# Two further matmuls behind each group of one-column modulation sums, in a one-core transformer kernel

## The chip, the cores and the metric

The kernel runs on one NeuronCore of a Trainium2 chip. The metric is device time in microseconds (us) of one execution, median of several. TensorE (PE) multiplies, VectorE (DVE) and ScalarE (ACT) prepare its operands and take its results out of PSUM, SyncE (SP) issues nearly all transfers from HBM.

## The reference, cut to what matters

Two transformer blocks run one after the other on 256 tokens of width 2048, batch 1, float32. The first block is a hybrid mixer (gated delta rule and convolution), cross attention to a memory of 256 tokens and a squared-ReLU MLP of width 8192. The second is a block whose norms and residuals are modulated by vectors that come from conditioning inputs:

```python
mod_in = jax.nn.silu(c)
modc_in = jax.nn.silu(c_ctx)
sh1, sc1, gt1, sh2, sc2, gt2 = jnp.split((mod_in @ w_mod[l] + b_mod[l])[:, None, :], 6, axis=-1)
csh1, csc1, cgt1, csh2, csc2, cgt2 = jnp.split(modc_in @ w_mod[l] + b_mod[l], 6, axis=-1)
h = rmsnorm(x, g_attn[l]) * (1 + sc1) + sh1
```

The matrix `w_mod` is 2048 x 12288 and multiplies single vectors, while every other matrix multiplies 256 tokens.

## The kernel before, in words

All dense layers are one stream. The weights of every layer lie in HBM as 906 slots of 128 x 1024 float32. SP loads a slot into one of 8 raw buffers. ACT rounds it to `whi` (float32r), DVE subtracts to get the remainder `wlo` (L1218), each with 4 buffers, and PE uses the slot in 24 matmuls of 256 columns: for each 128 x 128 block of weights the three products whi x act[0], whi x act[1] and wlo x act[0], where `act[0]` and `act[1]` are the rounded activations and their remainder. All of them are recorded at line L448. In nearly all phases the weights are the stationary operand and `act` (or `hid`, for the second matrix of an MLP) is the moving one. In phases marked `flip` (memv, nav_c, nav_x, v_c, v_x) they change places: `act` is stationary and `whi` or `wlo` is moving.

The phases follow each other in the order of `phases()`: glu, qkv, z, then the delta rule, wout, memk, memv, wq, cross attention, wo, then w1 and w2 four times, then the second block. PE waits at the start of a slot for `split_done` (the slot is rounded and subtracted) and at the start of a block of outputs for `block_free` (its PSUM bank, 0 or 1, was read).

The product with `w_mod` is done by DVE beside the phases memk to w2_3. These have two loop bodies each, of 16 slots or 384 matmuls, 24 bodies in all. In a body DVE accumulates 512 modulation columns into `modacc` (L1202, L1204), for both vectors in the first 8 bodies (`mod=2`) and for one in the other 16 (`mod=1`). What is left is a sum over the 128 partitions. PE does it in `mod_matmuls`, after slot 12 of the next body: 8 or 4 matmuls whose stationary operand is 128 columns of `modacc` and whose moving operand is one column of ones, into bank 2. They are plain float32, and each has two records in the trace. Behind them the last 3 slots (72 matmuls) of the body follow, then the next phase or body. Bank 7 isn't used in the phases of these bodies but for the attention behind wq, which overwrites what it reads.

`act_skew` (448 bytes) and `h_skew` (64 bytes) are unused columns of SBUF that shift `act` and what lies behind it against the weights' buffers.

Of the kernel before, what the change touches and what calls it, by code (L numbers as in the profile page):

```python
# [14 lines left out]
P = 128  # L15
D = 2048
T = 256
# [110 lines left out]
def build(nc, x_t, mem_t, ctx_t, stream, mods, pvec, eye, cmix, catt, na_bias, na_mask, out_t):  # L128
    es = ExitStack()
    with es:  # L130
        def sb(name, shape, dt=F32, stack=None):
            return (stack or es).enter_context(nc.sbuf_tensor(name, shape, dt))
# [9 lines left out]
        act = sb("act", [P, 2, DC, T], F32R)  # L142
# [14 lines left out]
        with ExitStack() as first:  # L157
# [9 lines left out]
            with ExitStack() as mlp:  # L167
                hid = sb("hid", [P, 2, DC, T], F32R, stack=mlp)
# [32 lines left out]
        bank = [es.enter_context(nc.psum_tensor(f"bank{i}", [P, 512], F32)) for i in range(8)]  # L201
# [217 lines left out]
        def _(pe):  # L419
            c = Counts(pe)  # L420

            def phase(ph, src, c0=0, after=None):
# [3 lines left out]
                def body(i):  # L426
                    for k in range(ph.K):
                        b = bank[(ph.block0 + k) % 2]

                        pe.wait_ge(block_free, i * ph.K + (ph.block0 + k + 1))  # L430
                        for sl in range(ph.slots_per_block):
                            j = k * ph.slots_per_block + sl

                            pe.wait_ge(split_done, i * ph.S + (ph.slot0 + j + 1 + RAW_N))
                            if after and k == 0:
                                c.at(after[0], after[1] + (sl + 1) * after[2])
                            buf = (ph.slot0 + j) % SPL_N
                            for ci in range(ph.per_slot):
                                kc = sl * ph.per_slot + ci
                                for hf in range(ph.ncol // P if not ph.flip else TT):  # L440
                                    for n, (wx, ax) in enumerate(((whi, 0), (whi, 1), (wlo, 0))):
                                        if ph.flip:
                                            lhs = src[:, ax, c0 + kc, hf * P:(hf + 1) * P]
                                            rhs = wx[:, buf, ci * NCOL:(ci + 1) * NCOL]
                                        else:
                                            lhs = wx[:, buf, ci * ph.ncol + hf * P:ci * ph.ncol + (hf + 1) * P]
                                            rhs = src[:, ax, c0 + kc, :]
                                        mm = pe.matmul(b[:, hf * T:(hf + 1) * T], lhs, rhs,  # L448
                                                       start=(kc == 0 and hf == 0 and n == 0),
                                                       stop=(kc == ph.chunks - 1 and n == 2), skip_group_check=True)  # L450
                            mm.then_inc(slot_used, 1)
                            if ph.mod and j == MOD_OUT_AT:
                                mod_matmuls(ph, i)
# [3 lines left out]
            def mod_matmuls(ph, i):  # L457

                mb = i + ph.mod0
                pe.wait_ge(mod_used, mb * 8 + (8 + MOD_N))  # L460
                for w in range(ph.mod):
                    for n in range(MOD_COL // P):
                        mm = pe.matmul(bank[2][:, 4 * w + n:4 * w + n + 1], modacc[:, w, n * P:(n + 1) * P],  # L463
                                       ones[:, 0:1], start=True, stop=True, skip_group_check=True)
                mm.then_inc(mod_out, 1)

            def row_sums(out, src, tok, start, stop):

                return pe.matmul(out, src[:, tok], ones[:, 0:1], start=start, stop=stop, skip_group_check=True)  # L469
# [55 lines left out]
            for q in range(DC // 4):  # L525
                c.at(normed, q + 1)
                for k in range(4 * q, 4 * q + 4):
                    for mt in range(TT):
                        mm = pe.matmul(bank[4][:, 16 * mt:16 * mt + 16], tmp[:, k, mt * P:(mt + 1) * P],
                                       cc(CM, "w_ba")[:, 16 * k:16 * k + 16], start=(k == 0 and mt == 0), stop=(k == DC - 1),  # L530
                                       skip_group_check=True)
# [258 lines left out]
            for n in range(1 + MLA_H // 2):  # L790
                src = kr[:, 0, :] if n == 0 else qR[:, n - 1, :]
# [1079 lines left out]
```

## Time and profile before

| | |
|---|---|
| median of 3 runs | 3073.99 us (3073.78, 3073.99, 3084.93) |
| the profiled execution, its own time | 3077.71 us |
| its span, first to last instruction | 3075.9 us |
| mean granted TensorE clock | 0.970 of 2.4 GHz |
| busy: PE, weight loads, DVE, ACT | 94%, 92%, 68%, 43% |
| HBM traffic | 588 MB, 192 GB/s over the span |

All durations below come from the one profiled execution, which lies 3.7 us above the median. A matmul's record is longer than its share of the stream, since consecutive ones overlap: the distance between starts is the pace, and the length of a record is more than twice as long.

### The profile page before, as it was taken

The numbers are of one execution on the slowest core, as the hardware profiler recorded it, in microseconds if no ns is written. First come the engines' busy times: TensorE is split into PE (matmuls) and PEld (weight loads), VectorE is DVE, ScalarE is ACT, GpSimd is POOL, SyncE is SP. The second block draws the span as 40 slices with busy tenths as digits, with TensorE's granted clock in tenths as the row PEclk, the third lists the DMA queues.
The fourth block names the chain that finished last, engine by engine and source line by source line (L and its number), as shares of the span: only waits on it lengthen the run. The fifth ranks groups of instructions, "written<-read, shape, count | busy, mean of one in ns | idle before, by whom it ended". The sixth has DMA issues, their size and how long they took to land.

```text
span 3075.9 us, 55206 instructions
## 1 busy us (share of the span) xinstructions
PE 2901.8 (94%) x23858; PEld 2838.5 (92%) x23858; DVE 2096.0 (68%) x2934; ACT 1331.7 (43%) x1646; POOL 5.1 (0%) x13
## 2 busy tenths in 40 slices
PE   7998888999999899999999989988998999999998
PEld 7998787999998899999999979967598999999998
DVE  6988654698977877676766775454457665665665
ACT  4445323443433453444435444434345543554453
POOL 0000000000000000000000000000000000000000
PEclk9999898999999999999999989998999999999999
DMA  5554102577664677777777745522144565555553
GB/s 203 188 169 165 55 1 80 204 254 260 245 227 168 240 289 275 280 274 268 287 268 267 282 140 178 190 98 96 55 156 153 195 199 196 191 195 196 192 195 117
DMA packets 160451, 591.58 MB, mean 192 GB/s; under 512 B 17840, under 2 KB 17840, under 8 KB 159696
## 3 DMA queue, kind: packets, MB, share of 16 engines
q1 hardware_dynamic: 159264, 579.93, 53.4%
q0 software_dynamic: 944, 8.12, 0.7%
q8 instruction: 188, 3.08, 0.4%
q14 instruction: 55, 0.45, 0.1%
HBM read 585.88 MB, written 2.10 MB: 191 GB/s over the span
## 4 chain that ended last, share of the span: by engine, by line
PE 86%; DVE 10%; ACT 2%; issue 1%; DMA 1%; SPq 0%; DVEq 0%; ACTq 0%
PE bank L448 76%; DVE wlo L1218 2%; PE bank L712 1%; DVE ev L1237 1%; DVE modacc L1423 1%; PE bank L469 1%; PE bank L463 1%; PE bank L616 1%; PE bank L473 1%; DVE tmp L1373 1%; PE bank L614 1%; PE bank L608 1%; DVE ev L1340 1%; PE bank L687 1%; ACT whi L823 1%
## 5 line engine op out<-in xcount | busy, mean ns | idle before, releaser
L448 PE MATMUL bank<-act,whi 128*128 128x256 f32 x10144 | 1784.4, 281 | 59.7 <-DVE wlo L1218 20.2
L448 PEld LDWEIGHTS bank<-act,whi 128*128 128x128 f32 x10144 | 1560.0, 191 | 65.4 <-issue 34.1
L1218 DVE TENSOR_TENSOR wlo<-raw,whi 128x1024 fp32r<-128x1024 f32 x906 | 1098.1, 1223 | 530.2 <-ACT whi L823 528.4
L448 PE MATMUL bank<-act,wlo 128*128 128x256 f32 x5072 | 1421.7, 280 | 0.0
L823 ACT ACTIVATE whi<-raw 128x1024 fp32r<-128x1024 f32 x906 | 948.2, 1057 | 898.0 <-PE bank L448 897.4
L448 PEld LDWEIGHTS bank<-act,wlo 128*128 128x128 f32 x5072 | 969.4, 191 | 0.0
L448 PE MATMUL bank<-hid,whi 128*128 128x256 f32 x3456 | 602.5, 279 | 0.0
L448 PEld LDWEIGHTS bank<-hid,whi 128*128 128x128 f32 x3456 | 524.5, 188 | 0.0
L448 PE MATMUL bank<-hid,wlo 128*128 128x256 f32 x1728 | 482.1, 279 | 0.0
L1204 DVE SCALAR_TENSOR_TENSOR modacc<-modraw,small,modacc 128x512 f32<-128x512 f32 x480 | 348.6, 747 | 11.0 <-DMA modraw<-mods 5.6
L448 PEld LDWEIGHTS bank<-hid,wlo 128*128 128x128 f32 x1728 | 328.8, 190 | 0.0
L448 PE MATMUL bank<-whi,act 128*128 128x256 f32 x896 | 158.1, 279 | 0.0
L448 PEld LDWEIGHTS bank<-whi,act 128*128 128x128 f32 x896 | 136.5, 188 | 0.0
L448 PE MATMUL bank<-wlo,act 128*128 128x256 f32 x448 | 125.0, 279 | 0.0
L1293 DVE SCALAR_TENSOR_TENSOR ev<-bank,pv,ev 128x255 f32<-128x255 f32 x176 | 76.9, 478 | 62.8 <-ACT ev L888 61.3
L1423 DVE SCALAR_TENSOR_TENSOR modacc<-modraw,modacc 128x256 f32<-128x256 f32 x232 | 98.6, 481 | 0.1
L448 PEld LDWEIGHTS bank<-wlo,act 128*128 128x128 f32 x448 | 84.1, 188 | 0.0
L888 ACT ACTIVATE ev<-bank,pv 128x256 f32<-128x256 f32 x88 | 45.0, 561 | 70.4 <-PE bank L448 70.4
L901 ACT ACTIVATE ev<-h 128x512 f32<-128x512 f32 x40 | 25.3, 632 | 113.6 <-DVE h L1268 68.0
L1282 DVE TENSOR_TENSOR hid<-ev,hid 128x512 fp32r<-128x512 f32 x32 | 22.2, 693 | 72.8 <-ACT hid L877 72.8
L893 ACT ACTIVATE ev<-ev 128x256 f32<-128x256 f32 x44 | 18.4, 419 | 80.1 <-DVE ev L1293 80.1
L1014 ACT ACTIVATE tmp<-bank 128x512 f32<-128x512 f32 x28 | 16.7, 597 | 73.6 <-PE bank L608 73.6
(269 smaller groups left out, 1545.3 us busy)
## 6 DMA issues: line engine op xcount, KB each, us to landing
raw<-stream SPq DMA_DIRECT2D x906, 512.0 KB, 4.4
modraw<-mods SPq DMA_DIRECT2D x192, 512.0 KB, 4.1
h<-x_t SPq DMA_DIRECT2D x4, 512.0 KB, 6.3
memV<-mem_t POOLq DMA_DIRECT2D x1, 2048.0 KB, 8.6
tmp<-ctx_t POOLq DMA_DIRECT2D x1, 2048.0 KB, 12.5
out_t<-tmp SPq DMA_DIRECT2D x4, 512.0 KB, 2.6
cz<-catt POOLq DMA_DIRECT2D x1, 1216.0 KB, 12.2
bias<-na_bias POOLq DMA_DIRECT2D x1, 1024.0 KB, 5.1
```

Of the source, the lines that this page charges most:

```text
L448: mm = pe.matmul(b[:, hf * T:(hf + 1) * T], lhs, rhs, start=(kc == 0 and hf == 0 and n == 0), stop=(kc == ph.chunks - 1 and n == 2), skip_ ...
L463: mm = pe.matmul(bank[2][:, 4 * w + n:4 * w + n + 1], modacc[:, w, n * P:(n + 1) * P], ones[:, 0:1], start=True, stop=True, skip_group_che ...
L469: return pe.matmul(out, src[:, tok], ones[:, 0:1], start=start, stop=stop, skip_group_check=True)
L473: return pe.matmul(out, small[:, col + n:col + n + 1].to_broadcast([P, P]), ident[:, :], start=start, stop=True, skip_group_check=True)
L608: mm = pe.matmul(bk(hg, 0)[:, n, :], MT[hg][:, n, :], X[hg][:, n, :], start=True, stop=True)
L614: pe.matmul(bk(hg, 2)[:, n, :], XT[hg][:, n, :], Y[hg][:, n, :], start=True, stop=True)
L823: sc.activation(whi[:, at % SPL_N, :], raw[:, at % RAW_N, :], ACT.Copy).then_inc(hi_done, 1)
L888: ins = sc.activation(ev[:, 0, hf * T:(hf + 1) * T], b2(b)[:, hf, :], ACT.Identity, scale=par("ff_conv", n * 6 + (6 * first + 3 * hf + 1)) ...
L1204: ins = ve.scalar_tensor_tensor(acc, wt, col, acc, ALU.mult, ALU.add)
L1218: ve.tensor_tensor(wlo[:, at % SPL_N, :], raw[:, at % RAW_N, :], whi[:, at % SPL_N, :].bitcast(F32), ALU.subtract).then_inc(split_done, 1)
L1293: ins = ve.scalar_tensor_tensor(o, b2(b)[:, hf, so], par("ff_conv", n * 6 + (6 * first + 3 * hf + j)), o, ALU.mult, ALU.add)
L1423: ins = ve.scalar_tensor_tensor(acc, x_, w, acc, ALU.mult, ALU.add)
```

## The change

Behind each group of one-column sums, after its semaphore has been signalled, two more matmuls are issued. Their stationary operand is one half of the first chunk of the activations that the phase at hand uses (`act`, or `hid` in a w2 phase). Their moving operand is 256 float32r columns of the same tensor, beginning at column 32, 128 bytes behind the place where the stream's own moving operands begin; it ends 32 columns inside the next chunk. They write bank 7, with start and stop set, and nothing reads the result. There is no wait and no signal on them. With 24 groups that is 48 matmuls more on PE, and nothing else is changed.

```diff
                         mm = pe.matmul(bank[2][:, 4 * w + n:4 * w + n + 1], modacc[:, w, n * P:(n + 1) * P],
                                        ones[:, 0:1], start=True, stop=True, skip_group_check=True)
                 mm.then_inc(mod_out, 1)
+                src = hid if ph.name.startswith("w2") else act
+                flat = src[:, 0, :, :].rearrange("p c t -> p (c t)")
+                for n in range(2):
+                    pe.matmul(bank[7][:, 0:T], src[:, 0, 0, n * P:(n + 1) * P], flat[:, P // 4:P // 4 + T], start=True, stop=True, skip_group_check=True)
```

## Rows read from the trace of the kernel before

**Rows 1.** The page: busy shares, and the granted clock in 40 slices.
```profile
PE 2901.8 (94%) x23858; PEld 2838.5 (92%) x23858; DVE 2096.0 (68%) x2934; ACT 1331.7 (43%) x1646; POOL 5.1 (0%) x13
...
PEclk9999898999999999999999989998999999999999
```

**Rows 2.** The page: the chain that ended last, by line.
```profile
PE bank L448 76%; DVE wlo L1218 2%; PE bank L712 1%; DVE ev L1237 1%; DVE modacc L1423 1%; PE bank L469 1%; PE bank L463 1%; PE bank L616 1%; PE bank L473 1%; DVE tmp L1373 1%; PE bank L614 1%; PE bank L608 1%; DVE ev L1340 1%; PE bank L687 1%; ACT whi L823 1%
```

**Rows 3.** Timeline of PE around the first group: start us, us, what.
```profile
652.79 0.39 PE L448 MATMUL bank<-act,whi 128*128 128x256 f32 x2
...
653.13 0.39 PE L448 MATMUL bank<-act,whi 128*128 128x256 f32 x2
...
653.47 1.84 PE L463 MATMUL bank<-ones,modacc 128*128 128x1 f32 x16
655.17 0.48 PE L448 MATMUL bank<-act,whi 128*128 128x256 f32 x2
...
655.96 0.40 PE L448 MATMUL bank<-act,whi 128*128 128x256 f32 x2
...
656.32 0.40 PE L448 MATMUL bank<-act,whi 128*128 128x256 f32 x2
```

**Rows 4.** L448 by duration, 1090.2 to 1134.9: ns min/median/max of a record.
```profile
L448 PE MATMUL bank<-act,whi x255: 281/281/364, 1089.9 to 1134.8; 128*128 128x256 f32 x128
```

**Rows 5.** L448 by duration, 2400 to 2500.
```profile
L448 PE MATMUL bank<-act,whi x590: 276/276/276, 2399.9 to 2500.0; 128*128 128x256 f32 x197
```

**Rows 6.** Windows: us, busy and count of each engine, PEclk, DMA share, GB/s.
```profile
626.00:653.00 27.00, 27.00 (x240) 27.00 (x240) 26.32 (x34) 12.17 (x14) 0.00 (x0) 1.00 0.87 314
982.00:1029.01 47.01, 47.01 (x402) 47.01 (x401) 44.69 (x58) 19.32 (x21) 0.00 (x0) 1.00 0.76 276
1135.07:1181.19 46.12, 46.12 (x394) 46.12 (x393) 33.76 (x39) 19.09 (x20) 0.00 (x0) 1.00 0.76 276
2344.00:3060.60 716.60, 716.60 (x6323) 716.60 (x6322) 463.94 (x635) 337.42 (x406) 0.00 (x0) 1.00 0.56 186
```

**Rows 7.** Groups of PE from 1090.2 to 1780.7: busy us, mean ns.
```profile
L448 PE MATMUL bank<-hid,whi 128*128 128x256 f32 x2000 | 354.4, 281 | 0.0
```

**Rows 8.** Timeline of PE around the ninth group.
```profile
1088.95 0.28 PE L448 MATMUL bank<-act,wlo 128*128 128x256 f32 x1
1089.07 0.95 PE L463 MATMUL bank<-ones,modacc 128*128 128x1 f32 x8
1089.88 0.48 PE L448 MATMUL bank<-act,whi 128*128 128x256 f32 x2
1090.20 0.28 PE L448 MATMUL bank<-act,wlo 128*128 128x256 f32 x1
```

**Rows 9.** Timeline of PE at the end of nav_c, a flip phase.
```profile
1885.87 0.40 PE L448 MATMUL bank<-whi,act 128*128 128x256 f32 x2
...
1886.57 0.39 PE L448 MATMUL bank<-act,whi 128*128 128x256 f32 x2
```

**Rows 10.** The same at the end of nav_x.
```profile
1963.08 0.39 PE L448 MATMUL bank<-whi,act 128*128 128x256 f32 x2
...
1963.77 0.40 PE L448 MATMUL bank<-act,whi 128*128 128x256 f32 x2
```

**Rows 11.** The same at the end of v_c.
```profile
2131.84 0.40 PE L448 MATMUL bank<-whi,act 128*128 128x256 f32 x2
...
2132.54 0.40 PE L448 MATMUL bank<-act,whi 128*128 128x256 f32 x2
```

**Rows 12.** The same at the end of v_x.
```profile
2154.46 0.40 PE L448 MATMUL bank<-whi,act 128*128 128x256 f32 x2
...
2155.16 0.39 PE L448 MATMUL bank<-act,whi 128*128 128x256 f32 x2
```

**Rows 13.** Timeline of PE at a wait in qkv, idle time in brackets.
```profile
182.98 0.50 PE L448 MATMUL bank<-act,whi 128*128 128x256 f32 x2 [1.49 <-DVE wlo L1218]
...
183.44 0.40 PE L448 MATMUL bank<-act,whi 128*128 128x256 f32 x2
```

**Rows 14.** The same at a later wait in qkv.
```profile
219.75 0.50 PE L448 MATMUL bank<-act,whi 128*128 128x256 f32 x2 [0.62 <-DVE wlo L1218]
...
220.56 0.39 PE L448 MATMUL bank<-act,whi 128*128 128x256 f32 x2
```

**Rows 15.** Waits from 1054 to 1780: total us, times, longest.
```profile
DVE wlo L1218 <- ACT whi L823: 104.8, 121, 1.6
```

## The prediction

> **What bounds the kernel now.** I read the page first: PE is busy in 94% of the span and holds its full clock in most slices [rows 1], and the chain that ended last runs for 76% over the stream's matmuls at L448 [rows 2]. So what a stream matmul costs, start to start, decides the time, and I went to PE's timeline for it, around the first of the 24 groups of sums. Ahead of it two pairs of whi matmuls start at 652.79 and 653.13: three matmuls in 0.340 us, 113.3 ns each. Behind it they start at 655.96 and 656.32: about 0.353 us for three, 118 ns each [rows 3]. Same kind of matmul, same operands, same full clock, no wait. The records are longer as well, 0.39 us for an overlapped pair before and 0.40 after.
>
> The view of one line by duration makes this a marker. From 1090 to 1135 every record of L448 but the first lasts 281 ns [rows 4]; from 2400 to 2500 all last 276 ns, minimum and maximum alike [rows 5]. The windows give the paces. From 2344 to 3060.6 there are 6,323 matmuls in 716.6 us, 113.3 ns each [rows 6]. A body of w1 or w2, from the last matmul ahead of a group to the same place one group on, takes 46.12 us [rows 6]. Of this 0.93 us lie from there to the first stream matmul behind the group [rows 8], 0.20 us to the second (1090.20 starts the third, one normal step behind it), and 382 steps are left: (46.12 - 1.13) / 382 = 117.8 ns. So the stream has two paces, 4.44 ns or 3.9% apart, and keeps each for hundreds of us. I call them the short and the long one.
>
> Where does it change? By the timeline all 24 groups leave the long pace, whatever was there ahead of them. Between groups nothing restores the short one but a rest of PE: the whole MLP, 1090 to 1781, runs at a mean of 281 ns [rows 7].
>
> **The change part by part.** *Signals and banks.* The pair stands behind the signal to DVE, writes a bank nobody reads and waits for nothing: 0. It is no load for ACT, DVE or SP. It reads `act` or `hid` while the phase still reads them, so no buffer is held longer: 0.
>
> *The pair itself.* Behind a group the first two wide matmuls start 0.20 us apart instead of 0.118 [rows 8]. This step is paid now by the stream and would then be paid by the pair. What is added is two ordinary steps. The trace has no such matmul with a shifted start; the nearest rows bound a step by 0.113 and 0.118 us, so a pair by 0.227 and 0.236 us, and if the step out of the pair is a wide one again, 0.20, it is 0.32. I take 0.23: 24 x 0.23 = +5.5 us, bounds +5.4 and +7.7.
>
> The Trainium skill ("TensorE: Matmul & The Clock Gate", Back-to-back issue gap) gives a warm isolated gap of N / 2.4 + 2.5 ns, an estimate of 109 ns for 256 columns. By it alone the pair would be 48 x 0.109 = +5.2 us and there would be one warm pace, with nothing to win back; the two paces of the trace, 113.3 and 117.8 ns at the same granted clock, don't agree with one gap.
>
> *What the pair does to the pace.* This is the unknown. The pace is not a property of the operands: the same phase runs at either, as the body before and after the first group does [rows 3]. It is a way in which weight loads and matmuls have locked to each other. Something that shifts one against the other by some ns can tip it. What tips it in the trace: (a) A wait. Of 10 waits at full clock inside the stream 5 were left in the short pace and 5 in the long one, as at 183 [rows 13] and 220 [rows 14]. (b) The end of a flip phase, without any wait. There `act` has been stationary, the moving columns began elsewhere (in `whi`), and the stream takes up `whi` as stationary and `act` as moving. Of four such seams three changed the pace: long to short at 1886 and 2155 [rows 9, 12], short to long at 1963 [rows 10]; the one at 2132 kept the long one [rows 11]. (c) The one-column group itself, always to long.
>
> The new pair makes the conditions of (b) right behind (c): `act` or `hid` stationary, moving columns that begin at another offset, then back to weights stationary and `act` moving. At entry the lock is the group's long one, and from the long one two of three such seams led to the short pace. Ends of the unknown: nothing is restored, 0; all is restored. The count for the latter: from each group to the next group or to the next rest of PE. Twenty bodies run from group to group (3 among the first four groups, 1 each in wq and wo, 15 in the MLP) with 382 long steps, and four tails of 71 steps end at a rest: 20 x 382 + 4 x 71 = 7,924 steps x 4.44 ns = -35.2 us. I take all of it, since by the seams this is the nearer row, and since the groups leave the same lock each time, so that what the pair does once it should do in nearly all.
>
> *Would the others keep up?* In the MLP DVE is busy 33.8 of 46.12 us and waits for ACT's rounding, which waits for PE [rows 6, 15]; a body shorter by 1.5 us leaves over 10 us of slack. The tightest body is one of wo, DVE 44.69 of 47.01 us [rows 6]; at the short pace it would last about 45.5 us. Cover is 0.8 us there, and if it were gone a body would lose a microsecond or so. Transfers ran at 314 GB/s in a short-paced stretch [rows 6], above the some 285 that the faster bodies would ask for. 0.
>
> **Sum.** -35.2 + 5.5 = -29.7 us. On the profiled execution 3077.7 - 29.7 = 3048.0; the median of the runs is 3.7 lower, so 3074.0 - 29.7 = **3044.3 us**, -1.0%.
>
> **Rivals.**
> 1. *The pair leaves the long pace* (chance 0.32). For it: all groups lead there, the wide step of 0.20 us may set the lock at the pair, and what follows it, including a seam like 2132 [rows 11], need not move it. Against: two seams of three. Then 3074.0 + 5.5 = 3079.5, +0.2%, the same within what a measurement can tell (about 0.5%, 15.4 us). The skill's page "SBUF — State Buffer" (Who interferes with whom) speaks for this rival: it says that PE never waits for anyone on its SBUF ports, by which the place where moving columns begin could not matter and 3079.5 would stand. That three seams without a wait changed the pace speaks against it; no row shows where the 4.44 ns are lost.
> 2. *It works for one of the two sources only* (chance 0.11), since `act` and `hid` lie at different places. If only the `act` groups restore it, the 8 w2 groups' bodies stay long: 8 x 382 x 4.44 = 13.6 us less, 3074.0 - 21.6 + 5.5 = 3057.9, -0.5%, on the line between faster and same.
> 3. *Slower, by a later lock* (chance 0.05). The last stretch, 6,323 matmuls from 2344 [rows 6], begins after a rest with a lock that could as well have been the long one. If the shifted timing gives it that, it costs 6,323 x 4.44 = 28.1 us: 3107.6 if the pair restores nothing. It passes the 0.5% at 15.4 - 5.5 = 9.9 us, 2,230 steps. With the pair working it gives 3072.4, the same.
>
> The forecast has 0.52. Its own range is 3037 to 3053: the stretches with a lock by chance, those in qkv and from 1790 to 2240, can each come out otherwise. The range for 8 in 10 must take in rival 1 with its bound of 7.7 us: 3038 to 3082. Faster takes the forecast (0.50 of it) and most of rival 2 (0.07): 0.57. Slower takes rival 3: 0.06, with a little for a pair that costs more than the bounds. The same is left with 0.37.
>
> **What would show each step.** Records of L448 behind a group would last 276 ns, not 281, and a body of the MLP would take about 44.7 us. If they last 281, rival 1 holds and a body takes 46.35 us. The two shifted matmuls should stand 0.20 us apart, the stream's first 0.11 to 0.12 us behind them. If w1 bodies show 276 and w2 bodies 281, it is rival 2; 281 from 2344 on would be rival 3. Waits of PE for `wlo` in wo would show the cover gone. The prediction is wrong if the lock is made by the one-column sums' lasting effect rather than by the step out of them, or if the pair tips the pace once for each of its two matmuls and so back.

## The result, and the profile after

Over 20 runs of each the median went from 3077.57 to 3050.41 us; the ratio is 0.9913, with a 95% interval of 0.9888 to 0.9938. That is 0.9% faster, and clear of no change. The forecast was 3044.3 us from a median of 3073.99, so -29.7 us; -27.2 us were measured, and the time lies in the forecast's own range of 3037 to 3053. Four of the 20 runs of either kernel lie some 30 us above the rest (3104.8 to 3110.6 before, 3078.6 to 3081.1 after); the experiments show one way to such a distance.

The page of the kernel after, to hold against [rows 1]; its profiled execution took 3043.18 us, with a span of 3041.4 us:

```profile
PE 2866.8 (94%) x23906; PEld 2803.7 (92%) x23906; DVE 2093.6 (69%) x2934; ACT 1329.0 (44%) x1646; POOL 5.1 (0%) x13
```

PE has 48 matmuls more and 35 us less of busy time. The other engines' work is unchanged. This execution is the fastest of the 20, and its span is 34.5 us shorter than the one before, more than the medians differ by. By the two timelines 7.7 us of this lie ahead of the first group (653.4 against 645.7 us), where the kernels are the same; that part is not the change's. From the first group to the 24th PE took 1127.4 us before and 1100.3 after, which is 27.1 us less, and behind the 24th 0.3 us more. The stretch in which anything was changed accounts for the difference of the medians.

PE's timeline around the ninth group of the kernel after, against [rows 8]:

```profile
1076.88 0.48 PE L469 MATMUL bank<-act 128*128 128x256 f32 x2
1077.19 0.40 PE L448 MATMUL bank<-act,whi 128*128 128x256 f32 x2
1077.43 0.28 PE L448 MATMUL bank<-act,wlo 128*128 128x256 f32 x1
1077.55 0.39 PE L448 MATMUL bank<-act,whi 128*128 128x256 f32 x2
```

The pair (L469) takes the wide step of 0.20 us, the stream starts 0.11 us behind its second matmul, and after one overlapped pair of 0.40 us the records are at 0.39. The body that follows, by duration, against [rows 4]:

```profile
L448 PE MATMUL bank<-act,whi x248: 276/276/276, 1077.9 to 1119.8; 128*128 128x256 f32 x124
```

All records last 276 ns where they lasted 281. The same holds to the end of the MLP. Groups of PE from 1077.5 to 1770, against [rows 7] (busy us, mean ns):

```profile
L448 PE MATMUL bank<-hid,whi 128*128 128x256 f32 x2048 | 348.9, 276 | 0.0
L448 PE MATMUL bank<-act,whi 128*128 128x256 f32 x1839 | 313.4, 276 | 0.0
```

Three windows of the kernel after (us, then busy time and count of each engine), a w1 or w2 body, the tightest body of wo, and the last stretch, against [rows 6]:

```profile
1120.61:1165.28 44.67, 44.67 (x396) 44.67 (x395) 33.88 (x39) 19.03 (x20) 0.00 (x0) 1.00 0.79 288
971.00:1016.34 45.34, 45.34 (x402) 45.34 (x401) 44.34 (x57) 18.15 (x21) 0.00 (x0) 1.00 0.76 270
2310.00:3026.00 716.00, 716.00 (x6320) 716.00 (x6319) 463.19 (x633) 337.11 (x405) 0.00 (x0) 1.00 0.57 187
```

A body fell from 46.12 to 44.67 us, PE stayed busy without a gap in wo although DVE was at 98%, and the last stretch was in the short pace before and after (716.0 / 6,320 = 113.3 ns).

The one place where it did not work is memv, a flip phase, between its first group and its second:

```profile
L448 PE MATMUL bank<-whi,act 128*128 128x256 f32 x239 | 42.3, 279 | 0.0
```

Its records last 279 ns, which is the long pace with exchanged roles (the record length differs by 1 or 2 ns there, the step is 117.8 ns as elsewhere). The timeline says where the short pace was lost: at the four float32 records of the norm's spreading (L477), issued between memk's last matmul and memv's first.

```profile
701.21 0.39 PE L448 MATMUL bank<-act,whi 128*128 128x256 f32 x2
...
701.55 0.60 PE L477 MATMUL bank<-ident,small 128*128 128x128 f32 x4
...
702.35 0.40 PE L448 MATMUL bank<-whi,act 128*128 128x256 f32 x2
```

Two things failed here, then: the short pace was lost at these records, and the pairs behind both groups of memv (at 739 and 786) did not bring it back. The traces of the experiments bear out the first: in all seven of the traces in which memk ended in the short pace, this one included, the four records turned it long.

### The profile page after: what moved, and what is told of

Same layout as the page of the kernel before. It is cut to its first block, busy times and chain, and to the rows that moved or that the text cites. A ratio compares the mean times of both kernels' runs of the same rounds, so it can differ in the third digit from the quotient of the medians.

```text
span 3041.4 us, 55302 instructions
## 1 busy us (share of the span) xinstructions
PE 2866.8 (94%) x23906; PEld 2803.7 (92%) x23906; DVE 2093.6 (69%) x2934; ACT 1329.0 (44%) x1646; POOL 5.1 (0%) x13
## 4 chain that ended last, share of the span: by engine, by line
PE 87%; DVE 10%; ACT 2%; issue 1%; DMA 0%; SPq 0%; DVEq 0%; ACTq 0%
PE bank L448 77%; DVE wlo L1222 2%; PE bank L716 1%; DVE ev L1241 1%; DVE modacc L1427 1%; PE bank L463 1%; PE bank L620 1%; PE bank L473 1%; DVE tmp L1377 1%; PE bank L618 1%; PE bank L477 1%; PE bank L612 1%; DVE ev L1344 1%; PE bank L691 1%; ACT whi L827 1%
## 5 line engine op out<-in xcount | busy, mean ns | idle before, releaser
L448 PE MATMUL bank<-act,whi 128*128 128x256 f32 x10144 | 1761.2, 279 | 62.1 <-DVE wlo L1222 23.1
L448 PEld LDWEIGHTS bank<-act,whi 128*128 128x128 f32 x10144 | 1550.1, 190 | 67.3 <-issue 34.1
L448 PE MATMUL bank<-act,wlo 128*128 128x256 f32 x5072 | 1413.6, 279 | 0.0
L448 PEld LDWEIGHTS bank<-act,wlo 128*128 128x128 f32 x5072 | 964.1, 190 | 0.0
L448 PE MATMUL bank<-hid,whi 128*128 128x256 f32 x3456 | 588.4, 276 | 0.0
L448 PEld LDWEIGHTS bank<-hid,whi 128*128 128x128 f32 x3456 | 520.3, 188 | 0.0
L448 PE MATMUL bank<-hid,wlo 128*128 128x256 f32 x1728 | 477.0, 276 | 0.0
L448 PEld LDWEIGHTS bank<-hid,wlo 128*128 128x128 f32 x1728 | 324.4, 188 | 0.0
L448 PE MATMUL bank<-whi,act 128*128 128x256 f32 x896 | 157.5, 279 | 0.0
L448 PEld LDWEIGHTS bank<-whi,act 128*128 128x128 f32 x896 | 136.4, 188 | 0.0
L448 PE MATMUL bank<-wlo,act 128*128 128x256 f32 x448 | 124.8, 279 | 0.0
L448 PEld LDWEIGHTS bank<-wlo,act 128*128 128x128 f32 x448 | 84.0, 188 | 0.0
```

The source lines that it names most:

```text
L448: mm = pe.matmul(b[:, hf * T:(hf + 1) * T], lhs, rhs, start=(kc == 0 and hf == 0 and n == 0), stop=(kc == ph.chunks - 1 and n == 2), skip_ ...
```

## The experiments

Each has the changed kernel as its base unless it says otherwise. Times are to be held against runs of the kernel before that were taken beside them: a median of 3078.8 us (7 runs) for the pair without the shift, the two other shifts and the one matmul behind the group; 3075.3 (one run) for the odd place, the one matmul and the pair in the middle, and the four matmuls; 3079.2 (one run) for the one-column matmul with a pair and for the 448 bytes taken out; 3078.0 (11 runs) for `act` moved alone and for the last kernel. Where a body's time is given, it is the distance between the last stream matmuls ahead of two neighbouring groups of the MLP, as for the 46.12 of [rows 6]. That a group or a pair leaves a pace means that this pace follows behind it.

### The pair without the shift

```diff
-                    pe.matmul(bank[7][:, 0:T], src[:, 0, 0, n * P:(n + 1) * P], flat[:, P // 4:P // 4 + T], start=True, stop=True, skip_group_check=True)
+                    pe.matmul(bank[7][:, 0:T], src[:, 0, 0, n * P:(n + 1) * P], flat[:, 0:T], start=True, stop=True, skip_group_check=True)
```

> The pair stays, but its moving columns begin at column 0 as the stream's do. Theory A, the shifted start of the moving columns is what tips the lock: the stream stays in the long pace behind every group, L448 records of 281 ns in the MLP, a body of w1 or w2 of about 46.35 us, and the whole about 3079 us. Theory B, any two wide matmuls that take the 0.20 us step out of the one-column group restore the pace, or a change of the stationary operand from activations to weights does: bodies of 44.67 us and about 3050 us, as with the shift.

Measured: 3050.5 us (4 runs, 3042.94 to 3053.55), ratio 0.988 (0.981 to 0.995), bodies of 44.65 us. Theory A fell at once: the shift is not what restores the pace. In memv the unshifted pair is even the better one. The same stretch between its two groups, by duration, with 276 ns where the shifted pair leaves 279:

```profile
L448 PE MATMUL bank<-whi,act x242: 276/276/276, 744.9 to 785.9; 128*128 128x256 f32 x121
```

### The stationary columns shifted instead, and a shift of 256 bytes

The line of the pair becomes, in the first and in the second kernel:

```diff
+                    pe.matmul(bank[7][:, 0:T], flat[:, n * P + P // 4:(n + 1) * P + P // 4], flat[:, 0:T], start=True, stop=True, skip_group_check=True)
```
```diff
+                    pe.matmul(bank[7][:, 0:T], src[:, 0, 0, n * P:(n + 1) * P], flat[:, P // 2:P // 2 + T], start=True, stop=True, skip_group_check=True)
```

> The pair with its stationary columns beginning 128 bytes on instead of its moving ones. If only where the moving columns begin matters: 281 ns and bodies of 46.35 us, like the pair without a shift. If the distance between the two operands' places matters, with either sign: 276 ns and 44.67 us.

> The pair with its moving columns beginning 256 bytes on instead of 128. If any other start will do: 276 ns, bodies of 44.67 us, 3045 to 3050 us for the whole. If the lock needs this one offset: 281 ns and 46.35 us, about 3079 us.

Measured: 3054.81 and 3052.03 us (one run each), MLP bodies of 44.66 and 44.65 us. All four variants of the pair restore the short pace in the MLP. In memv the 256-byte shift does it too, and the shifted stationary operand does not (279 ns again). So outside the flip phase the operands' place within the pair decides nothing, and inside it something depends on it, in no order that these four show.

### One matmul instead of two

```diff
-                for n in range(2):
+                for n in range(1):
```

> One shifted matmul instead of two. If the tipping happens at the step from shifted to unshifted moving columns (theory A in its simplest form), one is enough: bodies of 44.55 us, records of 276 ns. If the second is needed because the first one only carries the wide step of 0.20 us, the stream stays at 281 ns and a body lasts about 46.24 us.

Measured: 3071.76 us (one run). Neither expectation: in the MLP the groups now leave the short and the long pace in turn. Two neighbouring bodies, by duration:

```profile
L448 PE MATMUL bank<-act,whi x249: 276/276/277, 1089.8 to 1131.9; 128*128 128x256 f32 x125
...
L448 PE MATMUL bank<-hid,whi x202: 281/281/281, 1142.3 to 1177.8; 128*128 128x256 f32 x101
```

Bodies take 44.55 and 46.24 us by turns. One matmul makes the count in a body odd, so either the parity of something decides, or what the group leaves depends on the pace ahead of it: short becomes long and long becomes short. Outside memv all 22 groups of this trace left the opposite of the pace ahead of them, also behind rests of PE; the two in memv stayed long. The next two runs take the parity alone.

### An odd place for the group; one matmul far from it

Both start from the kernel before, without a pair. In the first the group is issued three matmuls earlier, inside the last chunk of slot 12. In the second one unshifted wide matmul stands behind slot 4 of each body.

```diff
+                                    if ph.mod and j == MOD_OUT_AT and ci == ph.per_slot - 1 and hf == 0:
+                                        mod_matmuls(ph, i)
```
```diff
+                            if ph.mod and j == 4:
+                                for n in range(1):
+                                    pe.matmul(bank[7][:, 0:T], src[:, 0, 0, n * P:(n + 1) * P], src[:, 0, 0, :], start=True, stop=True, skip_group_check=True)
```

> No matmul is added; the group is issued three matmuls (an odd number) earlier, inside the last chunk of slot 12. Theory P, with the parity of the place deciding and nothing else: 113.3 behind each group, bodies of 44.4 us, about 3038 us. If parity of the place is nothing to it: 117.8, bodies of 46.12 us, the time of before.

> No pair behind the groups; instead one unshifted wide matmul with activations stationary after slot 4 of each body, far from the group. It makes the count of matmuls in a body odd. Theory P, the pace behind a group is set by whether an odd or even number of matmuls has gone by: the groups leave the long and the short pace in turn (117.8, 113.3, 117.8, ...), as with one matmul behind each group. Theory M, the group always leaves the long pace and a single wide matmul turns whatever pace it finds into the other: every group leaves 117.8, and the matmul after slot 4 turns it to 113.3, so that a body has about 286 steps of 113.3 up to the next group (of 24 x 12 less 96, and 72 + 120 of 117.8).

Measured: 3081.32 and 3084.84 us (one run each). All groups leave the long pace in both, though the second has odd bodies. Mean record of the hid matmuls over the MLP, first the odd place, then the single matmul:

```profile
L448 PE MATMUL bank<-hid,whi 128*128 128x256 f32 x1996 | 353.7, 281 | 0.0
```
```profile
L448 PE MATMUL bank<-hid,whi 128*128 128x256 f32 x1998 | 354.4, 281 | 0.0
```

The parity alone does not decide it. The single matmul never turned the long pace into the short one either, against theory M; but the two times that it met the short pace it turned it long. One of these, by duration ahead of and behind the inserted matmul at 1070:

```profile
L448 PE MATMUL bank<-act,whi x55: 276/276/276, 1060.3 to 1069.4; 128*128 128x256 f32 x55
...
L448 PE MATMUL bank<-act,whi x108: 281/281/281, 1070.9 to 1089.8; 128*128 128x256 f32 x108
```

### The pair in the middle of the stream, without and with a one-column matmul

Again from the kernel before. First the unshifted pair alone behind slot 4, then with one one-column float32 matmul (two records) ahead of it, the second line below, which the first kernel lacks:

```diff
+                            if ph.mod and j == 4:
+                                pe.matmul(bank[7][:, T:T + 1], ident[:, :], ones[:, 0:1], start=True, stop=True, skip_group_check=True)
+                                for n in range(2):
+                                    pe.matmul(bank[7][:, 0:T], src[:, 0, 0, n * P:(n + 1) * P], src[:, 0, 0, :], start=True, stop=True, skip_group_check=True)
```

> No pair behind the groups; the unshifted pair stands after slot 4 of each body instead. Theory S, the seam out of the pair (activations stationary, then weights stationary) restores the short pace wherever it stands: 117.8 from the group to slot 4, 113.3 from there to the next group, about half of the gain, 3060 to 3066 us. Theory G, the pair works only right behind the group, where it takes the wide step of 0.20 us: 117.8 throughout and about 3079 us.

> Behind slot 4 of each body, where the pair alone had restored nothing, one one-column float32 matmul (two records) goes ahead of the unshifted pair; the groups have no pair. Theory L, the short pace needs a loss of lock by one-column matmuls (weight loads set the pace, 112 ns, and the next wide step is 0.20 us) and then the pair: 276 ns from slot 4 to the next group, about 192 steps of 113.3 in a body of the MLP, which lasts about 45.4 to 45.9 us against 46.35 with the pair alone. Rival: a single one-column matmul is not enough, or what counts is something else of the groups (their place behind slot 12, their count): 281 ns throughout.

Measured: the pair alone restores nothing, and the three times that it met the short pace the long one followed; the records from slot 4 to the next group last 280 to 282 ns, and the run took 3111.35 us. With the one-column matmul ahead of it: 3073.17 us, bodies of 45.75 us, and the pace turns at this very place. Behind slot 4 of the first w1 body that follows a group:

```profile
L448 PE MATMUL bank<-act,whi x109: 281/281/281, 1089.9 to 1108.9; 128*128 128x256 f32 x109
```
```profile
L448 PE MATMUL bank<-act,whi x114: 276/276/276, 1111.8 to 1131.0; 128*128 128x256 f32 x114
```

So it needs both, one-column matmuls and a pair behind them. (In memv, the flip phase, the short medicine did nothing.) There is a price: in the three bodies in which this short medicine met the short pace (at 628, 957 and 1063) it left the long one. A whole group with a pair has no such memory: the unshifted pair came out short from the long pace (groups at 741, 976 and 1080 of its run) and from the short one (all others).

The 3111.35 us of the pair alone are not its own: its MLP is in the long pace, as before, and so is the last stretch from 2349, which is in the short one in the trace before. The next run shows the same in a kernel whose pairs work.

### Four matmuls, unshifted, halves of the stationary chunk by turns

```diff
-                for n in range(2):
-                    pe.matmul(bank[7][:, 0:T], src[:, 0, 0, n * P:(n + 1) * P], flat[:, P // 4:P // 4 + T], start=True, stop=True, skip_group_check=True)
+                for n in range(4):
+                    pe.matmul(bank[7][:, 0:T], src[:, 0, 0, n % 2 * P:(n % 2 + 1) * P], flat[:, 0:T], start=True, stop=True, skip_group_check=True)
```

> Four unshifted matmuls behind each group instead of two. If only the seam counts, or an even number: 113.3 behind each group, bodies of about 44.88 us in the MLP. If each further matmul tips the pace and back, an even number also gives 113.3. If the pair is special, 117.8 and bodies of 46.6 us.

Measured: 3080.67 us (one run), MLP bodies of 44.91 us and 276 ns in them, as expected of the seam. In memv four unshifted matmuls did not restore the pace (280 ns), where two did. And the time is 30 us above that of the pair. The two further matmuls cost 0.24 us a body, under 6 us in all; the rest is in the last stretch, against [rows 5]:

```profile
L448 PE MATMUL bank<-act,whi x556: 281/281/281, 2399.9 to 2497.9; 128*128 128x256 f32 x186
```

From 2319 on it has 6,317 steps near 117.8 ns. That is 6,317 x 4.44 = 28.1 us, the price of the third rival, and nothing in the code there differs. The distance between the two clusters of runs noted above is 3080.6 - 3049.7 = 30.9 us after and 3105.7 - 3075.8 = 29.9 before (medians of the 4 and of the 16). No trace shows one of these eight executions, so that they are this stretch is inferred from the size.

### Where the operands lie

First the 448 unused bytes ahead of `act` are taken out. Then `act` alone is moved, with `hid` and all else in place:

```diff
-        sb("act_skew", [P, 112])
```
```diff
-        sb("act_skew", [P, 112])
+        sb("act_skew", [P, 64])                        (second)
-        sb("h_skew", [P, 16])
+        sb("h_skew", [P, 64])
```

> The changed kernel with the 448 unused bytes ahead of act taken out, so that act and all behind it lie elsewhere against the weights' buffers. Theory A, the two paces come from where the operands lie against each other: other paces than 113.3 and 117.8 ns, or only one of them, and another time by tens of us. Theory B, the paces are a matter of weight loads against matmuls in time alone: the same two paces, bodies of 44.67 us, and about 3050 us.

> The changed kernel with act placed 192 bytes lower (256 unused bytes ahead of it instead of 448) and 256 instead of 64 unused bytes behind it, so that h, hid and all else stay where they are. If the distance of moving and stationary operands sets the paces: the phases that stream act get other paces than 113.3 and 117.8, while the w2 and down phases, which stream hid, keep them. If only the distance modulo something coarser counts, or hid's place matters to both: no difference. Between no skew (120.0 ns everywhere) and 448 bytes I expect act phases at 117 to 120 ns, and the whole at 3080 to 3130 us.

Measured: 3170.76 and 3134.65 us (one run each). Without the skew there is one pace, 120.0 ns, in every phase, at the start, behind groups, behind waits; records last 283 ns, and bodies 47.20 us. The second run is the cleanest of the study: phases that stream `act` are at 120.0 ns, those that stream `hid` at 113.3, side by side at full clock.

```profile
L448 PE MATMUL bank<-act,whi x279: 283/283/283, 2399.9 to 2449.9; 128*128 128x256 f32 x140
...
L448 PE MATMUL bank<-hid,whi x237: 276/276/276, 2559.9 to 2600.0; 128*128 128x256 f32 x119
```

So what PE reads and where it lies sets its step; moving `act` left the weights' buffers where they were. At the skew of these kernels there are two stable steps, at the other two there is one, and it is the slowest of the three.

### The unshifted pair, and the same medicine at two more places

```diff
-                    pe.matmul(bank[7][:, 0:T], src[:, 0, 0, n * P:(n + 1) * P], flat[:, P // 4:P // 4 + T], start=True, stop=True, skip_group_check=True)
+                    pe.matmul(bank[7][:, 0:T], src[:, 0, 0, n * P:(n + 1) * P], src[:, 0, 0, :], start=True, stop=True, skip_group_check=True)
+                            if (ph.name, i, j) in (("up_0", 1, 0), ("cq", 0, 0)):
+                                for n in range(4):
+                                    pe.matmul(bank[7][:, T:T + 1], ident[:, :], ones[:, 0:1], start=True, stop=True, skip_group_check=True)
+                                kick(src)
```

`kick` issues the unshifted pair.

> The unshifted pair behind each group, and the same medicine (four one-column float32 matmuls, then the pair, 1.2 us) once in the first slot of cq and once in up_0 when the clock is full. Theory L: from 2,360 on all L448 records last 276 ns in every run, cq to fn too, so that the long-paced last stretch, which some runs of either kernel seem to have (those near 3080 of the changed kernel, 3105 of the one before), is gone: median about 3047, and no run above 3060. Rival: where the pace is short already, the medicine turns it long, as one one-column matmul with the pair did; then the last stretch would be at 281 ns in most runs, 3074 to 3078.

Measured: 3047.23 us (6 runs, 3045.8 to 3054.76), ratio 0.9894 (0.985 to 0.994) to the kernel before. At both added places (1936 and 2337) the short pace was there already in the profiled run, and it was kept, so the rival fell. With four one-column matmuls ahead the medicine does not turn the short pace, as it did with one. No run of the six is near 3080, but with 4 in 20 of the changed kernel there that happens by chance in a quarter of such sets (0.8 to the sixth), so that the late cases are gone isn't shown. Against the changed kernel's 3050.41 the gain is 3 us, within what these runs can tell. Memv is in the short pace in it (276 ns).

## Why the prediction was right, and where its reason was not

*Two paces, 4.44 ns apart, decide.* Right. Short-paced steps rose from some 11,100 to some 18,700 of some 21,700 (told apart by record length). Between the first group and the 24th they rose from 581 to 7,910; 7,329 x 4.44 ns = 32.5 us less, and 5.5 us for the pairs, give -27.0 of the 27.1 us there. Of the 35 us by which PE's busy time fell, 27 lie in this stretch. That the pace is not a property of the operands holds at this one placement only: with `act` elsewhere its phases had the step of 120.0 ns and no other.

*The pair's price.* 0.23 us was taken; a w1 or w2 body was to last about 44.7 us with it and lasted 44.67. The fifteen MLP bodies gave 15 x 1.45 = 21.8 us.

*How much is restored.* All 24 groups were counted, 22 worked. What failed is the part of the term in memv: from 702 to 796 us some 765 steps stayed long, 3.4 us. The prediction had not looked at the four float32 records between memk and memv, where the pace was lost. It had also counted memv's two groups by its seam from activations to weights as stationary operand. In a flip phase there is no such seam, since the stream itself holds `act` stationary, and behind both shifted pairs the pace stayed long there. But that isn't the whole of it: the unshifted pair, which has no such seam either, did restore it. 1.3 us came back, since the 290 steps ahead of the first MLP group happened to start in the short pace this time. -35.2 + 3.4 - 1.3 + 5.5 = -27.6 us, against -27.1 in the stretch of the groups and -27.2 between the medians.

*Why the pair tips the pace.* Here the reason was only half right. The prediction took the seam from activations to weights as stationary operand for the tipping, by the rows at the ends of flip phases [rows 9 to 12]. At those ends the rows read well, and the experiments' traces add to them: over the twelve traces at this skew 42 of 48 such ends changed the pace (23 of 29 from long to short, all 19 from short to long). But in the middle of the stream the pair's own seam, without a group ahead of it, restored nothing. What does it is the one-column matmuls followed by the pair. Whether the pair must hold activations stationary isn't shown, since no run put two matmuls with the stream's own operands there; the nearest row is the stream itself, whose first two matmuls take the same wide step behind a plain group and stay in the long pace. What the prediction calls a lock is so far a pace that the stream keeps: no run shows that a shift of weight loads against matmuls tips it. And the shift, which the change seems to be about, does nothing for it.

*The others keep up.* Right: no wait of PE in wo, DVE 44.34 of 45.34 us.

*Rival 1* fell: the records behind 22 groups last 276 ns. "SBUF — State Buffer" of the Trainium skill (Who interferes with whom) says that PE never waits on any other engine at its SBUF ports, and the prediction concluded that place could not matter. Within the pair it didn't, outside memv. But moving `act` by 192 bytes cost its phases 6.7 ns a matmul, 120.0 against 113.3, so the conclusion does not hold; no run here shows whether these 6.7 ns are a wait at a port, and so the sentence itself is neither borne out nor refuted. *Rival 2* fell: `act` and `hid` groups behave alike. *Rival 3* was rightly priced at 28.1 us, and is real, but nothing shows that the change causes it: four executions in 20 have something of that size, with the pair and without (of 20 further runs of the kernel before, five, at 3101 to 3108 us).

The forecast of -29.7 us was near for the right reason in its size (two paces, the count of steps, the price of the pair), but that the pair would tip the pace at all rested on a row that turned out to be another case; there it was in part luck.

What stays open: where in PE the 4.44 ns are lost, why two matmuls behind a group end in the short pace and one in the opposite of the pace ahead, what is different in memv, and whether another skew has only the short one. Skews other than 0, 256 and 448 bytes weren't tried.

## What to carry to other kernels

In a dense matmul stream read the start-to-start step, not busy time: if one kind of matmul has two steps at the same clock, multiply the difference by the count before anything else. Look at what stood ahead of each turn (float32 one-column matmuls, norm spreads, waits, the end of a phase with exchanged operands) and try a cheap wide pair behind it. Vary the distance in SBUF between moving and stationary operands by some hundred bytes as well, since here the 448 bytes were worth four times as much as the pair (3170.8 against 3050.4 us).

## What was not expected of the hardware

- The step of a 256-column float32r matmul with its weight load was 113.3, 117.8 or 120.0 ns at the full 2.4 GHz, by the place of the operands and by what had gone before, and the first held for 716 us on end.
- Of two placements side by side in one execution, one gave 120.0 ns and the other 113.3, with the same instructions.
- Each of the two records of a one-column float32 matmul has a weight load of its own and takes a step of about 112 ns, nearly that of a 256-column matmul (the 16 records of a group 1.84 us). Behind them the first two wide matmuls start 0.20 us apart.
- Within a pace a weight load starts a fixed time ahead of its matmul: 110 ns in the short pace (2400 to 2500 of the trace before), 114 to 115 in the long one (1100 to 1130), 117 to 118 at 120.0 ns a step (without the skew). The weight loads of `wlo` last 188 ns in the first stretch and 192 in the other two.
- What one wide matmul behind a group leaves depends on the pace ahead of it: it gave the two paces in turn through the sixteen groups of the MLP.
- All 36 seams into a flip phase without other records between kept the pace, and 42 of the 48 out of one changed it, in twelve traces.
